# Differential attention: normalising the value product instead of the weights, and the next unit's first maximum placed ahead of the present unit's combination

## The reference, cut to what matters

```python
s = jnp.einsum('bqhmd,bkhmd->mbhqk', qblk, k) * scale      # two maps m, 64 wide each
p = jax.nn.softmax(s, axis=-1)
w = p[0] - lam * p[1]
o = jnp.einsum('bhqk,bkhe->bqhe', w, v)                    # 128 wide
...
a = rmsnorm(att, subln_g) * (1.0 - lam_init)               # over the 128 values of a head
```

## Time and profile before

| | us |
|---|---|
| median of 3 runs | 2036.97 |
| lowest and highest run | 2032.71, 2037.42 |
| the profiled execution's own time | 2038.92 |
| its span, first to last instruction | 2037.1 |
| attention stage, first scores to first output-projection matmul | 314.60 to 407.48 |
| mean granted TensorE clock over the span | 0.95 of 2.4 GHz |

### The profile page before, as it was taken

The page is one execution under the profiler, slowest core; times in us unless marked ns, Lnnn a source line. Parts: engine busy times, 40 slices in busy tenths (PEclk is TensorE's granted clock), DMA queues, the critical chain, the costliest instruction groups (busy, mean ns, idle before and its releaser), DMA issues.

```text
span 2037.1 us, 27726 instructions
## 1 busy us (share of the span) xinstructions
PE 1796.3 (88%) x8945; PEld 1453.2 (71%) x8945; DVE 1582.6 (78%) x3005; ACT 671.0 (33%) x1103; POOL 896.9 (44%) x718
## 2 busy tenths in 40 slices
PE   6999998798776666647999999999999999999992
PEld 1244445645776666646999999999999999999991
DVE  0312005523999999998999999999999999999986
ACT  1010014501154555522333333333333333333331
POOL 0200000000032323314888777887766666666660
PEclk9999998998998888878999999999999999999996
DMA  9731210150003333376999999999999999999992
GB/s 324 253 139 57 81 42 0 53 217 32 1 6 81 81 84 83 83 214 237 407 400 407 388 407 408 407 402 402 402 406 402 403 394 404 396 407 407 403 398 108
DMA packets 253466, 520.76 MB, mean 256 GB/s; under 512 B 113889, under 2 KB 130913, under 8 KB 252129
## 3 DMA queue, kind: packets, MB, share of 16 engines
q1 hardware_dynamic: 177952, 249.00, 34.8%
q0 software_dynamic: 73728, 268.47, 33.3%
q10 hardware_dynamic: 1730, 2.59, 0.4%
HBM read 488.54 MB, written 31.46 MB: 255 GB/s over the span
## 4 chain that ended last, share of the span: by engine, by line
PE 53%; DVE 24%; issue 14%; DMA 4%; ACT 4%; DVEq 1%; POOL 0%; SPq 0%; ACTq 0%; POOLq 0%
DVE arena L1089 10%; PE ps L1419 9%; PE ps L1418 9%; PE ps L1417 9%; PE ps L1200 7%; PE ps L1364 5%; PE ps L1392 4%; PE ps L1174 4%; PE ps L1344 3%; DVE V_lo L1051 2%; DMA U_in<-in_expert_uT 2%; PE ps L1242 1%; DMA arena_w<-in_w_mod 1%; DMA arena<-x_scratch 1%; DVE C_lo L1064 1%
## 5 line engine op out<-in xcount | busy, mean ns | idle before, releaser
L1417 PE MATMUL ps<-hT_hi,U_hi 128*128 128x384 f32 x1024 | 344.3, 336 | 36.3 <-DVE U_lo L1046 36.3
L1419 PE MATMUL ps<-hT_hi,U_lo 128*128 128x384 f32 x1024 | 344.3, 336 | 0.0
L1418 PE MATMUL ps<-hT_lo,U_hi 128*128 128x384 f32 x1024 | 343.7, 336 | 0.0
L1417 PE MATMUL ps<-V_hi,C_hi 128*128 128x512 f32 x768 | 300.5, 391 | 17.7 <-DVE C_lo L1064 17.7
L1419 PE MATMUL ps<-V_hi,C_lo 128*128 128x512 f32 x768 | 302.5, 394 | 0.0
L1418 PE MATMUL ps<-V_lo,C_hi 128*128 128x512 f32 x768 | 302.2, 394 | 0.0
L1417 PEld LDWEIGHTS ps<-hT_hi,U_hi 128*128 128x128 f32 x1024 | 192.8, 188 | 41.4 <-issue 36.5
L452 POOL DMA_INDIRECT arena<-in_expert_u,idxn x128 | 169.1, 1321 | 96.5 <-DVE arena L1078 34.2
L707 ACT CAST V_hi<-V_in 128x1024 fp32r<-128x1024 f32 x128 | 134.9, 1054 | 214.9 <-PE ps L1419 214.9
L452 POOL DMA_INDIRECT arena<-in_expert_v,idxn x128 | 159.3, 1245 | 92.2 <-DVE arena L1089 40.6
L715 ACT ACTIVATE act_t<-ps 128x384 f32<-128x384 f32 x128 | 63.0, 492 | 412.1 <-PE ps L1419 412.1
(11 more groups left out here) (213 smaller groups left out, 3251.4 us busy)
## 6 DMA issues: line engine op xcount, KB each, us to landing
U_in<-in_expert_uT SPq DMA_DIRECT2D x128, 512.0 KB, 9.1
V_in<-in_expert_v SPq DMA_DIRECT2D x128, 512.0 KB, 6.4
arena_w<-in_w_mod SPq DMA_DIRECT2D x12, 2048.0 KB, 8.3
gates_scratch<-arena_w SPq DMA_DIRECT2D x6, 4096.0 KB, 20.7
gate_in<-gates_scratch SPq DMA_DIRECT2D x128, 192.0 KB, 7.5
arena_w<-in_w_in SPq DMA_DIRECT2D x4, 2048.0 KB, 8.0
arena_w<-in_w_query SPq DMA_DIRECT2D x1, 7168.0 KB, 21.2
arena_w<-in_w_out SPq DMA_DIRECT2D x2, 2048.0 KB, 7.7
```

Of the source, the lines that this page charges most:

```text
L1417: nc.tensor.matmul(out, hi, rhi, start=start, stop=False)
L1418: nc.tensor.matmul(out, hi, rlo, start=False, stop=False)
L1419: return nc.tensor.matmul(out, lo, rhi, start=False, stop=stop)
```

## The change

The weights are left unnormalised up to the constant of the first map: the combination becomes one pass, `probs1 * factor + probs0`, whose factor is minus lambda times the first sum divided by the second. The reciprocal of the first sum is kept per head in a new tile `inv4` (two buffers by block). The unnormalised value product is squared and summed as before; `att_var` multiplies the sums twice by the reciprocals, and `att_norm` multiplies the inverse root once by them. `neg_max` is split into a call for each map, and in each pass the first map's maximum of unit i + 1, and `att_var`, now stand ahead of `combine(i)`; the second map's maximum stays behind it.

```diff
--- before.py
+++ after.py
@@ -128,6 +128,7 @@
         amax = sb("amax", [P, 2, 2])
         asum = sb("asum", [P, 2, 2])
         ss4 = sb("ss4", [P, 2, H])
+        inv4 = sb("inv4", [P, 2, 2, H])
         iota = sb("iota", [P, NKEY])
         places = sb("places", [P, TOPK], bf16)
         idx = sb("idx", [P, 2, SLOTS], u32)
@@ -844,46 +845,54 @@
 
             dve.wait_ge(s_lam, 1)
 
-            def neg_max(i):
+            def neg_max(i, m):
                 b, h = UNITS[i]
                 z_, n_ = (1, P) if b == 0 else (2, KEYS_S // 2)
-                for m in range(2):
-                    dve.wait_ge(s_scores, 2 * i + m + 1)
-                    if i >= 2:
-                        dve.wait_ge(s_exp, 2 * (i - 2) + m + 1)
-                    dve.tensor_reduce(amax[:, i % 2, m:m + 1], ps[:, 2 * m:2 * m + z_, 0:n_], AX.XY, ALU.max,
-                                      negate=True).then_inc(s_amax, 1)
+                dve.wait_ge(s_scores, 2 * i + m + 1)
+                if i >= 2:
+                    dve.wait_ge(s_exp, 2 * (i - 2) + m + 1)
+                dve.tensor_reduce(amax[:, i % 2, m:m + 1], ps[:, 2 * m:2 * m + z_, 0:n_], AX.XY, ALU.max,
+                                  negate=True).then_inc(s_amax, 1)
 
             def combine(i):
 
                 b, h = UNITS[i]
                 n_ = P if b == 0 else KEYS_S
                 dve.wait_ge(s_exp, 2 * i + 2)
-                link(dve.reciprocal(asum[:, i % 2, :], asum[:, i % 2, :]))
-                dve.tensor_tensor(asum[:, i % 2, 1:2], asum[:, i % 2, 1:2], lam[:, 5:6], ALU.mult)
+                inv = inv4[:, b % 2, :, h]
+                link(dve.reciprocal(inv, asum[:, i % 2, :]))
+                link(dve.scalar_tensor_tensor(out=inv[:, 1:2], in0=inv[:, 1:2], scalar=lam[:, 5:6],
+                                              in1=asum[:, i % 2, 0:1], op0=ALU.mult, op1=ALU.mult))
                 if i >= 2:
                     dve.wait_ge(s_wT, i - 1)
-                link(dve.tensor_scalar(Wt[:, i % 2, 0:n_], probs[:, i % 2, 0, 0:n_], asum[:, i % 2, 0:1], None, ALU.mult))
-                dve.scalar_tensor_tensor(out=Wt[:, i % 2, 0:n_], in0=probs[:, i % 2, 1, 0:n_], scalar=asum[:, i % 2, 1:2],
-                                         in1=Wt[:, i % 2, 0:n_], op0=ALU.mult, op1=ALU.add).then_inc(s_w, 1)
+                dve.scalar_tensor_tensor(out=Wt[:, i % 2, 0:n_], in0=probs[:, i % 2, 1, 0:n_], scalar=inv[:, 1:2],
+                                         in1=probs[:, i % 2, 0, 0:n_], op0=ALU.mult, op1=ALU.add).then_inc(s_w, 1)
 
             def att_var(b):
+
+                inv = inv4[:, b % 2, 0, :]
                 dve.wait_ge(s_asq, b + 1)
+                link(dve.tensor_tensor(ss4[:, 0, :], ss4[:, 0, :], inv, ALU.mult))
+                link(dve.tensor_tensor(ss4[:, 0, :], ss4[:, 0, :], inv, ALU.mult))
                 dve.tensor_scalar(ss4[:, 0, :], ss4[:, 0, :], 1.0 / P, EPS, ALU.mult, ALU.add).then_inc(s_avar, 1)
 
             def att_norm(b):
                 dve.wait_ge(s_arstd, b + 1)
+                link(dve.tensor_tensor(ss4[:, 1, :], ss4[:, 1, :], inv4[:, b % 2, 0, :], ALU.mult))
                 a = att.rearrange("p (h e) -> p h e", h=H)
                 dve.tensor_tensor(a, a, ss4[:, 1, :].unsqueeze(2).broadcast_to([P, H, P]), ALU.mult).then_inc(s_att, 1)
 
-            neg_max(0)
+            neg_max(0, 0)
+            neg_max(0, 1)
             for i in range(len(UNITS) + 2):
+                if i + 1 < len(UNITS):
+                    neg_max(i + 1, 0)
+                if i % H == 1 and i > H:
+                    att_var(i // H - 1)
                 if i < len(UNITS):
                     combine(i)
-                if i % H == 1 and i > H:
-                    att_var(i // H - 1)
                 if i + 1 < len(UNITS):
-                    neg_max(i + 1)
+                    neg_max(i + 1, 1)
                 if i % H == 1 and i > H:
                     att_norm(i // H - 1)
 
```

## The result

The changed kernel takes 2071.14 us (median of 4 runs, 2070.88 to 2072.88) against 2037.20 for the kernel before in the same comparison, so 34 us slower. The ratio is 1.0172 (of the means; 95% interval 1.0154 to 1.0190). The forecast was 2070. The profiled execution has a span of 2069.6 us.

A forecast was written before the change was run, and what follows sets the result against it. The prediction took the attention to be bound by a DVE-ACT-DVE ring of 4.21 us a unit, with no engine full. Long units and block ends +32.5, last unit -1.2, short units +2: +33.3 us, giving 2070 us, range 2049 to 2088.

The forecast's parts named there:

- the ring that the move closes: Attention: combination, PE's transposes, products and scores, then first maximum; a chain of two passes becomes one, 4.21 to 5.26 us.
- 5.26 us at full clock: Long attention unit at full clock: 1.81 + 1.38 + 0.73 + 0.40 + 0.94 us, against 4.21 before.
- 7.87 at half clock: Long attention unit at half clock: 1.12 + 2.14 + 2.54 + 0.73 + 0.40 + 0.94 us.
- The clock swings, taken halfway: PE's clock in the attention swings between full and half; middle of 5.26 and 7.87, 6.56 us a unit; chance 0.60.
- What makes it swing: PE busy only 61% at full clock lets the clock fall; busy 5.80 of 7.87 us at half clock, it rises.
- The blocks' ends: Three block ends: 0.2 us waiting, 0.48 small operations, 0.77 `attT` transposes; 3 x 1.4 = 4.2 us.
- The two ends of the stage: Attention's short units 0 to 3 cost +2 us; the last unit takes 3.0 us in place of 4.2, -1.2.
- The pass removed: Dropping L866 from DVE's combination shortens 0.86 us to 0.40, a gain of 0.46 us a unit.
- The delay passes through: Everything behind the attention stands in line, so the attention's +33.3 us reaches the kernel's end.
- The clock that holds: Rival: full clock throughout the attention, 5.26 us a unit, total 2050 us; chance 0.17.
- a faster kernel: Rival: the early maximum fills DVE's 1.00 us of idleness, 3.2 us a unit, total 2022 us; chance 0.04.
- Nothing to measure: Rival: PE's delay is swallowed, units stay near 4.21 us, total 2031 to 2043; chance 0.04.

The follow-up runs named there:

- first experiment: Changed kernel with DVE's order as before, combination and then both maxima, the new arithmetic kept: 2030.71 us, ratio 0.9974.
- second: Kernel before with only DVE's order changed, first maximum and `att_var` ahead of the two-pass combination: 2074.02 us, ratio 1.0192.
- third: Changed kernel with PE issuing the scores of unit i + 2 ahead of the products of unit i - 1: 2058.94 us, ratio 1.0110.
- fourth experiment: Changed kernel with six unread 128x128 identity matmuls a unit added on PE ahead of the weights' transposes: 2051.02 us, ratio 1.0075.
- the version with `att_var` behind: New arithmetic, old place of the maxima, `att_var` moved behind both maxima: 2029.50 us; with one filling matmul a unit 2029.91.

## Why the prediction was right, point by point

- *The bound now, and the ring that the move closes.* Right: in the changed kernel DVE waits for PE's scores in each long unit, PE for DVE's combination in 13, and the reciprocal no longer for ACT. Undoing the order alone takes the whole loss away (first experiment), making it alone brings the whole loss (second), and changing PE's list alone brings a part of it back (third).
- *5.26 us at full clock.* 5.32 measured. The small operation L864, of which no row existed, takes 0.26 to the next start where 0.20 was taken from L862; the other steps agree to 0.01.
- *7.87 at half clock.* Unit 5 (330.94 to 337.29, clock 0.51) confirms it in a shorter form. Its products go from 334.19 to the scores at 334.75, 0.56 us where five blocks of keys take 2.14; 7.87 less 1.58 is 6.29, and 6.35 was measured. Unit 6, at 0.54, takes 8.03 with the operations of `att_var` in it.
- *The clock swings, taken halfway.* That it swings was right; that the middle gave the time was in part luck, and the prediction said that no row stood for it. The mean came out at 6.90 us a unit against 6.56 + 0.30 for the blocks' ends, but hardly a unit looks like the middle. A plain unit takes 5.32 at full clock or 6.92 at 0.75, since the half clock falls on PE's busy part; the mean is pulled down by the short unit 5 and by two units at full clock. In the run with `att_var` put back only one was (clock 0.73).
- *What makes it swing.* From unit 5 to 19 PE is busy 66.7 of 96.7 us, 69%, between the 61% and 74% of the two ends. The 37 us at full clock in the trace of before were a poor guide: they had been measured with a PE idle for 17% of the time. The page of the Trainium skill that was weighed ("TensorE: Matmul & The Clock Gate", section "A second HAM failure mode: psum-queue depth-cycling"), which tells of a clock that swings where PE idles shortly between groups of matmuls, was the better guide here. This trace agrees with it: the units' clocks are 0.51 to 0.77 in twelve of the 14 long units and 1.00 in two. That idleness is the cause is shown by the fourth experiment, not by the page of the Trainium skill.
- *The blocks' ends, 1.4 us each, three times.* At full clock 0.61 for `att_var` (5.93 against 5.32; 0.68 forecast) and 0.44 for the transposes of `attT` (5.76 against 5.32; 0.77 had been taken, from a row at half clock). From unit 5 to 19 `att_var` comes four times and `attT` three times, so the sum should have had one more of the former; 4 x 0.61 + 3 x 0.44 = 3.8 against the 4.2 put down.
- *The two ends of the stage.* Here the sum was wrong twice, by -1.3 and +1.7 us, and the errors nearly cancel, which is luck. The start was put at +2: the first scores of unit 4 do come 1.5 us later (9.17 us from the stage's start in place of 7.69), but from there to the first maximum of unit 5 it is 6.00 us in place of 6.76, so +0.7 in all. The last unit was put at -1.2, and the time from its first maximum to the output projection is 15.37 us in place of 14.87, +0.5. The step that fails is "3.0 us in place of 4.2": the combination of unit 18 stands between the two maxima of unit 19, which the sum left out. From its first maximum to its last pass unit 19 takes 4.21 us (427.61 to 431.82), in the kernel before 3.40 (392.61 to 396.01).
- *The pass removed, 0.46 us a unit.* 0.41 where it can be seen by itself (4.21 to 3.80).
- *The delay passes through.* Right: 34.3 us in the stage, 34 in the total. Against the second trace of the kernel before the stage's part is 36.0, so this agrees to 2 us and no better.
- *The rivals.* The clock that holds was priced at 2050; the kernel in which it did hold took 2051.02. For a faster kernel the next scores would have had to be in PSUM while DVE was still busy or ACT at the second exponential; DVE idles 2.51 us for them even at full clock, and 4.54 in the unit ahead of the one shown, which holds `attT` and some half clock. The rival "Nothing to measure" was dismissed with a wrong size: by the terms of its neighbours a ring 0.5 us shorter, not 0.8, would have brought the total within 6.1 us of the kernel before. The measured ring leaves no room for either.

## What to carry to other kernels

Moving an instruction forward in an engine's own list also moves its wait, and everything behind it in that list then waits too. Before such a move, follow the released work around all engines, in the order of each list, and count over how many passes of the loop the chain was spread: here a chain of PE and DVE that had two passes was closed into one, and 4.21 us became 5.32, although the moved work was the same and the idle time it was meant to fill was there. Then ask what the new idle time does to TensorE's clock: here that was the larger part of the loss, 20 of 34 us.

## What the runs showed of the hardware

- Filling PE's wait with six 128x128 matmuls a unit (1.5 us of PE's time) whose result nobody reads brought the granted clock from 0.75 to 0.98 over the stage and the kernel from 2071 to 2051 us. In the old order two matmuls a unit moved the kernel before by 2 us, and one a unit the version with `att_var` behind by nothing that can be told.
- The old order depends less on the clock: 0.87, 0.93 and 0.95 over the stage went with 92.9, 91.2 and 90.8 us (kernel before, twice, and with filling).
- The granted clock can swing in a period in which PE is never idle for long: from unit 5 to 19 of the changed kernel no wait of PE is longer than 2.62 us, and the clock fell to half again and again; with the wait filled (PE busy 86% in place of 69%) it was 1.00 for 78 us. In the kernel before it fell once behind a stretch with PE busy 85%.
